# Compressed attention branch of a hybrid decoder block: PSUM copies moved from the vector to the scalar engine, two clamps replaced by a mask column, and low parts placed behind a weight split

## The chip, the cores and the metric

One core of a Trainium2 chip runs the kernel. Its engines work in parallel, each through its own queue in order: TensorE (PE in the profile, its weight loads PEld), VectorE (DVE), ScalarE (ACT), GpSimd (POOL), and SyncE (SP), which issues the DMAs. They are held together by semaphores that are written out by hand. The metric is device time in microseconds for one execution, as the median of several.

## The reference

One mixer layer: RMS norm, one input projection of 512 tokens x 1024 channels, three head groups, and one output projection added to the residual.

```
h = rmsnorm(x, norm_g)
proj = jnp.einsum('bsd,de->bse', h, w_in)
...
y_lru = rglru_group(...)     # gated linear recurrence
y_nsa = nsa_group(...)       # 8 query heads, 2 key/value heads
y_fox = fox_group(...)       # 8 heads, forget gates
y = jnp.concatenate([y_lru, y_nsa, y_fox], axis=-1)
return x + jnp.einsum('bse,ed->bsd', y, w_out)
```

The change touches the compressed branch of `nsa_group`. Its keys and values are made from 31 overlapping windows of 32 tokens. A query may see a window only when the window ends at or before it, so the first 31 queries see none and get zero:

```
k_cmp = rmsnorm(einsum(kc[:, tok] + pe_k, wck), k_g);  v_cmp = einsum(vc[:, tok] + pe_v, wcv)
s = jnp.einsum('bsgrd,bngd->bgrsn', qg, k_cmp) * ATTN_SCALE
s = jnp.where(mask, s, NEG_INF);  m = max(s);  e = jnp.where(mask, jnp.exp(s - m), 0.0)
p = e / jnp.maximum(jnp.sum(e), 1e-30)
o = jnp.einsum('bgrsn,bngd->bsgrd', p, v_cmp)
```

With 512 tokens there are 8 selection blocks of 64 and up to 16 may be selected, so the selected branch takes them all, and the importance scores need not be computed.

## The kernel before, in words

**Precision.** Every fp32 product with a weight is made of three matmuls on split operands: high x high, high x low and low x high. ACT copies a raw weight chunk to its high part (`split`, L513, 128x1024), then DVE subtracts to get the low part (`split_low`, L791). Queries and keys are treated alike: ACT writes the high part (`norm_high`, L589, two halves of 64 partitions), DVE the low part (L815, two halves).

**The stream of chunks.** The input projection runs over 39 chunks of 128 output channels (`CHUNKS`), in this order at the start: `u` x4 (recurrence input), `fg` (gate logits), `kc`, `vc` (input of the compressed keys and values), `ks`, `kw`, `nq` x4 (queries of the NSA group), `vn` x2 (token-major values), `zl` x4 (gates of the recurrence). Then comes the first attention (64 units of scores, exponent, transpose, values; TensorE lines L1232, L1241, L1260), 20 more chunks, the second attention, 4 chunks and the output projection. `project(c)` on TensorE makes a chunk with 24 matmuls (L1146 to L1148; for `vn` four units of 24 with 256 columns, L1126 to L1128). A chunk is read out of one of three PSUM banks, so a unit waits for the read of the unit three before it.

**Each engine has its own loop over the same chunks.** What stands in it by hand is the order of the engine's queue. Names for the order in one iteration `c`, before the change:

- ACT: exponent of the compressed scores (`zl` only, L670), `norm_seeds(c-1)` (four activations L521 to L524), `split(c+3)`, `before(c)` (square L545, or sigmoid L539 for `zl`), the first three reads of a `vn` chunk (`read_tokens`, L603), `norm_high(c-1)`, the fourth read; and after `nq3` the high part of the compressed keys (L704).
- DVE: `cmp_probs(t)` (`zl` only, L906 to L921), the read of chunk `c` (L769), `cmp_values` at `vn0` (L892), `after(c-1)` (L808 to L810 normalise, then the two low parts L815, which wait for ACT's high parts), `lru_tail` (L851 to L856 in two pieces), `cmp_norm` after `nq3` (L880 to L885), `cmp_transposed` (`zl` only, L930), `split_low(c+3)`.
- TensorE: `project(c)`; inside `zl0`, after half of its matmuls, `cmp_scores(0)` (L1192); after each `zl` chunk `t`: `cmp_transpose(t)` (L1201), `cmp_scores(t+1)`, `cmp_values(t)` (L1212). `cmp_transpose(t)` waits for DVE's `cmp_probs(t)`.

**The compressed branch, block t of 128 queries.** TensorE scores against high and low keys into one bank; DVE adds the mask and the two parts, takes the row maximum, clamps it, subtracts; ACT takes the exponent; DVE sums, clamps the sum, multiplies with the reciprocal and the gate; TensorE transposes into `PT[0]`; `cmp_transposed(t)` copies the 128x256 result to `std`; TensorE multiplies with `v_blocks`; `cmp_out_read(t)` copies the 128x512 output to `o_nsa`. `v_blocks` is block-diagonal, filled by `cmp_values` with eight copies of 32x64 out of PSUM. The clamps exist for rows without a visible window:

```
link(dve.tensor_scalar(mx, mx, NEG / 10, None, ALU.max))
link(dve.tensor_scalar(sm, sm, 1e-30, None, ALU.max))
```

`link` makes DVE wait for its own result. The compressed keys and values have 32 columns; column 31 is padding and zero in both. On ACT, sigmoid and the exponent set are in different tables; a switch is an instruction of its own (ACT_TABLE_LOAD).

## Time and profile before

| | |
|---|---|
| median of 3 runs | 458.04 us (457.46 to 458.3) |
| the profiled execution | 459.54 us, its span 457.7 us |
| TensorE, matmul | 434.9 us busy, 95% of the span |
| VectorE | 298.8 us, 65% |
| ScalarE | 255.7 us, 56% |
| GpSimd | 75.5 us, 16% |
| chain that ended last | PE 82%, DVE 9%, issue 3%, ACT 3%, DMA 2% |

The profile follows one execution. The chain of waits goes back from the last instruction, at each step to what released it; its shares tell on which engine the end of the kernel hung. The granted clock of TensorE is given as a share of full speed: 1.00 is 2.4 GHz and 0.50 is 1.2 GHz.

### The profile page before, as it was taken

What the parts mean: (1) busy time and instruction counts of PE and PEld (TensorE: products, weight loads), DVE (VectorE), ACT (ScalarE), POOL (GpSimd) and SP (SyncE); (2) the same over time, 40 slices, a digit from 0 to 9 for tenths busy, and PEclk for the clock granted to TensorE, in tenths of its full rate; (3) what the DMA queues carried; (4) which work ended last, traced back from release to release, by engine and by line L of the source; (5) the groups of instructions that cost most, each with busy time, mean ns of one, the idle gap of its engine ahead of it and who ended that gap; (6) DMA issues with size and microseconds to landing.
All of it is one profiled execution on the core that took longest, in us unless ns stands there. A gap on an engine that the chain in (4) does not pass through costs nothing.

```text
span 457.7 us, 6527 instructions
## 1 busy us (share of the span) xinstructions
PE 434.9 (95%) x2232; PEld 333.5 (73%) x2232; DVE 298.8 (65%) x631; ACT 255.7 (56%) x496; POOL 75.5 (16%) x122
## 2 busy tenths in 40 slices
PE   5899999999859989999999999999799999999997
PEld 1477688777848866676667897898577778888885
DVE  5975549887797998767427863857886448722204
ACT  4645695468734577878718873862487635311100
POOL 3002240000000036666500000000166300000000
PEclk9899999999997999999999999999999999999999
DMA  7822333432121210000011225372400012832004
GB/s 248 328 92 86 99 94 92 139 92 92 47 92 48 92 47 3 1 1 2 1 46 48 92 70 161 95 204 71 134 5 1 1 47 95 280 132 92 1 0 183
DMA packets 12961, 39.52 MB, mean 86 GB/s; under 512 B 1792, under 2 KB 2048, under 8 KB 12672
## 3 DMA queue, kind: packets, MB, share of 16 engines
q1 hardware_dynamic: 12928, 39.11, 26.5%
q8 instruction: 18, 0.29, 0.3%
q14 instruction: 15, 0.12, 0.1%
HBM read 32.81 MB, written 2.10 MB: 76 GB/s over the span
## 4 chain that ended last, share of the span: by engine, by line
PE 82%; DVE 9%; issue 3%; ACT 3%; DMA 2%; SPq 1%; POOL 0%; DVEq 0%; ACTq 0%; POOLq 0%
PE bank L1146 12%; PE bank L1148 12%; PE bank L1147 12%; PE bank L1260 6%; PE bank L1241 6%; PE bank L1363 5%; PE bank L1361 5%; PE bank L1362 5%; PE bank L1232 3%; PE bank L1233 3%; PE bank L1157 2%; PE bank L1126 2%; PE bank L1176 2%; PE bank L1128 2%; PE bank L1127 2%
## 5 line engine op out<-in xcount | busy, mean ns | idle before, releaser
L1146 PE MATMUL bank<-xh,wh 128*128 128x512 f32 (+1 forms) x264 | 112.4, 426 | 0.0
L1148 PE MATMUL bank<-xh,wl 128*128 128x512 f32 (+1 forms) x264 | 104.1, 394 | 0.0
L1147 PE MATMUL bank<-xl,wh 128*128 128x512 f32 (+1 forms) x264 | 103.5, 392 | 0.0
L791 DVE TENSOR_TENSOR wl<-raw,wh 128x1024 fp32r<-128x1024 f32 x51 | 62.0, 1219 | 30.2 <-ACT wh L513 29.8
L513 ACT ACTIVATE wh<-raw 128x1024 fp32r<-128x1024 f32 x51 | 53.0, 1049 | 29.6 <-PE bank L1363 27.0
L1146 PEld LDWEIGHTS bank<-xh,wh 128*128 128x128 f32 (+1 forms) x264 | 49.7, 188 | 14.6 <-issue 4.6
L1147 PEld LDWEIGHTS bank<-xl,wh 128*128 128x128 f32 (+1 forms) x264 | 49.7, 188 | 14.6 <-issue 4.2
L1148 PEld LDWEIGHTS bank<-xh,wl 128*128 128x128 f32 (+1 forms) x264 | 49.3, 187 | 11.8
L987 DVE CUSTOM_DVE_ANT_0 bank<-bank,mask_row 128x256 f32<-128x256 f32 (+3 forms) x96 | 46.8, 499 | 14.0 <-PE bank L1233 13.4
L481 POOL TENSOR_SCALAR probs<-probs,rcp,gates 128x384 f32<-128x384 f32 (+3 forms) x44 | 27.2, 628 | 115.4 <-DVE rcp L1003 115.3
L1363 PE MATMUL bank<-wh,yl 128*128 128x512 f32 x96 | 37.8, 394 | 0.0
L1361 PE MATMUL bank<-wh,yh 128*128 128x512 f32 x96 | 37.8, 394 | 0.0
L1362 PE MATMUL bank<-wl,yh 128*128 128x512 f32 x96 | 37.8, 394 | 0.0
L634 ACT ACTIVATE probs<-bank,negmax 128x256 f32<-128x256 f32 (+3 forms) x64 | 33.7, 530 | 5.3 <-DVE negmax L987 5.2
L644 ACT ACTIVATE pT<-bank 128x384 f32<-128x384 f32 (+1 forms) x48 | 26.1, 546 | 13.3 <-PE bank L1241 12.8
L1241 PE MATMUL bank<-cst,probs 128*128 128x128 f32 x160 | 28.4, 278 | 1.8 <-POOL probs L481 0.8
L1126 PE MATMUL bank<-wh,xh 128*128 128x256 f32 x96 | 28.5, 297 | 1.3 <-ACT v_nsa L603 1.3
L1127 PE MATMUL bank<-wl,xh 128*128 128x256 f32 x96 | 26.8, 280 | 0.0
L1128 PE MATMUL bank<-wh,xl 128*128 128x256 f32 x96 | 26.8, 280 | 0.0
L769 DVE TENSOR_TENSOR qr<-bank,rstd_bc 128x512 f32<-128x512 f32 (+1 forms) x19 | 13.1, 688 | 20.0 <-PE bank L1148 19.9
L1232 PE MATMUL bank<-kh_nsa,q_nsa 128*128 128x256 f32 (+3 forms) x64 | 25.1, 395 | 0.9 <-ACT probs L634 0.9
L1241 PEld LDWEIGHTS bank<-cst,probs 128*128 128x128 f32 x160 | 18.5, 140 | 7.4 <-POOL probs L481 3.3
(208 smaller groups left out, 786.2 us busy)
## 6 DMA issues: line engine op xcount, KB each, us to landing
raw<-in_w_in SPq DMA_DIRECT2D x39, 512.0 KB, 3.4
raw<-in_w_out SPq DMA_DIRECT2D x12, 512.0 KB, 3.4
x_raw<-in_xT SPq DMA_DIRECT2D x8, 256.0 KB, 6.1
x_res<-in_x_tok SPq DMA_DIRECT2D x1, 2048.0 KB, 9.6
out_y<-y_out SPq DMA_DIRECT2D x8, 256.0 KB, 2.1
cmp_w_sb<-in_cmp_w SPq DMA_DIRECT2D x1, 1024.0 KB, 9.9
kh_fox<-kh_fox SPq DMA_DIRECT2D x8, 128.0 KB, 2.3
kl_fox<-kl_fox SPq DMA_DIRECT2D x8, 128.0 KB, 2.4
```

Of the source, the lines that this page charges most:

```text
L513: act.activation(wh[:, c % HL, :], raw[:, c % RAW, :], ACT.Copy).then_inc(wh_ready, 1)
L791: dve.tensor_tensor(wl[:, c % HL, :], raw[:, c % RAW, :], wh[:, c % HL, :].bitcast(F32), ALU.subtract).then_inc(wl_ready, 1)
L987: dve.tensor_tensor_reduce(scores, scores, mask_row[:, SEQ - n:], scale=-1.0, scalar=3.0e38, op0=ALU.add, op1=ALU.min, accum_out=negmax[:, ...
L1126: pe.matmul(dst, xh[:, k, toks], hi[:, k], start=(k == 0), stop=False)
L1146: pe.matmul(dst, hi, xh[:, k, :], start=(k == 0), stop=False)
L1147: pe.matmul(dst, hi, xl[:, k, :], start=False, stop=False)
L1148: mm = pe.matmul(dst, lo, xh[:, k, :], start=False, stop=(k == KT - 1))
L1232: pe.matmul(dst[:, 0:n], q, kh[:, 0:n], start=(group == "nsa"), stop=False)
L1241: mm = pe.transpose(PT[u % PTB][:, cols], probs_of(u, j * P, (j + 1) * P), ident)
L1361: pe.matmul(dst, yh[:, e, toks], wh[:, c % HL, cols], start=(e == 0), stop=False)
L1362: pe.matmul(dst, yh[:, e, toks], wl[:, c % HL, cols], start=False, stop=False)
L1363: mm = pe.matmul(dst, yl[:, e, toks], wh[:, c % HL, cols], start=False, stop=(e == ET - 1))
```

## The change

Four edits. (1) `cmp_values` (8 copies), `cmp_transposed` (4 copies) and `cmp_out_read` (4 copies) go from DVE to ACT. The eight stand behind `split` of iteration `vn0` and ahead of the reads of that chunk; `cmp_transposed(t)` stands behind `split` and ahead of the sigmoid of `zl` chunk `t`; `cmp_out_read(t-1)` stands behind the exponent of block `t`, the last one in step 7 of the first attention. (2) The two clamps go. Instead, the mask's padding column 31 holds -1e29 in place of -1e30: the row maximum is then never under -1e29, and a row without a visible window has its whole weight on the padding column, whose value is zero. (3) On DVE, `after` is cut in two: `split_low(c+3)` now stands between the normalisation and the two low parts (`after_low`), in both loops over chunks. (4) `cmp_scores(0)` stands behind two of the eight channel tiles of chunk `zl0`, not four.

```
@@ -564,6 +564,28 @@
+            def cmp_values():
+                act.wait_ge(v_cmp_T, 1)
+                for g in range(KVH):
+                    for r in range(GROUP):
+                        act.activation(v_blocks[32 * r:32 * r + 32, g, r * HD:(r + 1) * HD],
+                                       AUX_B[0:CMP_PAD, g * HD:(g + 1) * HD], ACT.Copy).then_inc(v_cmp_ready, 1)
+            def cmp_transposed(t):
+                act.wait_ge(cmp_pT, t + 1)
+                if t >= 1:
+                    act.wait_ge(cmp_o, t)
+                act.activation(std[:, 0:2 * P], PT[0][:, 0:2 * P], ACT.Copy).then_inc(cmp_pT_sb, 1)
+            def cmp_out_read(t):
+                act.wait_ge(cmp_o, t + 1)
+                act.activation(o_nsa[:, :, t * P:(t + 1) * P],
+                               OUT[t % 2][:, :].rearrange("p (i q) -> p i q", i=HEADS // 2),
+                               ACT.Copy).then_inc(cmp_o_read, 1)
             def norm_seeds(c):
@@ -637,6 +659,8 @@
                 for s, inside in steps(first, last):
+                    if s == 7:
+                        cmp_out_read(NT - 1)
                     u = inside(s - T_LAG)
@@ -668,9 +692,15 @@
                     act.activation(p, p, ACT.Exp).then_inc(cmp_exp, 1)
+                    if t >= 1:
+                        cmp_out_read(t - 1)
                 if c >= 1:
                 split(c + AHEAD)
+                if CHUNKS[c][0] == "zl":
+                    cmp_transposed(CHUNKS[c][1])
+                if c == AT["vn", 0]:
+                    cmp_values()
                 before(c)
@@ -809,6 +839,10 @@
                                              ALU.mult).then_inc(normed, 1)
+            def after_low(c):
+                if c in NORMED:
+                    n = nth_normed(c)
                     for s in range(2):
@@ -884,13 +918,6 @@
                                       ALU.subtract).then_inc(k_cmp_ready, 1)
-            def cmp_values():
-                dve.wait_ge(v_cmp_T, 1)
-                for g in range(KVH):
-                    for r in range(GROUP):
-                        dve.tensor_copy(v_blocks[32 * r:32 * r + 32, g, r * HD:(r + 1) * HD],
-                                        AUX_B[0:CMP_PAD, g * HD:(g + 1) * HD]).then_inc(v_cmp_ready, 1)
@@ -907,32 +934,16 @@
                 link(dve.tensor_reduce(mx, p3, AX.X, ALU.max))
-                link(dve.tensor_scalar(mx, mx, NEG / 10, None, ALU.max))
                 dve.tensor_tensor(p3, p3, mx.unsqueeze(2).broadcast_to([P, HEADS, CMP_PAD]),
                 if t >= 1:
-                    cmp_out_read(t - 1)
                     lru_output(t - 1)
                 link(dve.tensor_reduce(sm, p3, AX.X, ALU.add))
-                link(dve.tensor_scalar(sm, sm, 1e-30, None, ALU.max))
                 link(dve.reciprocal(rc, sm))
                                   ALU.mult).then_inc(cmp_p, 1)
-            def cmp_transposed(t):
-                dve.wait_ge(cmp_pT, t + 1)
-                if t == 0:
-                    dve.wait_ge(normed, 6)
-                if t >= 1:
-                    dve.wait_ge(cmp_o, t)
-                dve.tensor_copy(std[:, 0:2 * P], PT[0][:, 0:2 * P]).then_inc(cmp_pT_sb, 1)
-            def cmp_out_read(t):
-                dve.wait_ge(cmp_o, t + 1)
-                dve.tensor_copy(o_nsa[:, :, t * P:(t + 1) * P],
-                                OUT[t % 2][:, :].rearrange("p (i q) -> p i q", i=HEADS // 2)).then_inc(cmp_o_read, 1)
@@ -972,8 +983,6 @@
                 for s, inside in steps(first, last):
-                    if s == 7:
-                        cmp_out_read(NT - 1)
                     if s == 16:
@@ -1060,18 +1069,16 @@
                     cmp_out(1)
-                if c == AT["vn", 0]:
-                    cmp_values()
                 if c >= 1:
                     after(c - 1)
+                split_low(c + AHEAD)
+                if c >= 1:
+                    after_low(c - 1)
                 for i, step in enumerate(TAIL_AT):
                     cmp_norm()
-                if CHUNKS[c][0] == "zl":
-                    cmp_transposed(CHUNKS[c][1])
-                split_low(c + AHEAD)
             attention(0, NSA_UNITS)
@@ -1081,6 +1088,7 @@
                 split_low(c + AHEAD)
+                after_low(c - 1)
             attention(NSA_UNITS, UNITS)
@@ -1138,7 +1146,7 @@
                         head_mean(c - 1)
-                    if k == KT // 2 and c == AT["zl", 0]:
+                    if k == 2 and c == AT["zl", 0]:
                         cmp_scores(0)
@@ -1425,6 +1433,7 @@
         c[:, CMPMASK + t * CMP_PAD:CMPMASK + (t + 1) * CMP_PAD] = np.where(seen, 0.0, NEG)
+        c[:, CMPMASK + t * CMP_PAD + N_CMP] = NEG / 10
     return c```

**DVE, from the normalisation of `nq2` to the first mask addition of the compressed branch (iterations `nq3`, `vn0`, `vn1`).** `wl` is the low weight part, `q_nsa` the low query parts, `k_cmp_*` the norm of the compressed keys. Before:

```order
L810 SCALAR_TENSOR_TENSOR qr<-qr,chn,std 128x512
L815 TENSOR_TENSOR q_nsa<-qr,q_nsa 64x512 x2
L880 TENSOR_TENSOR k_cmp_sq<-k_cmp_sq,k_cmp_w 64x64
L881 SCALAR_TENSOR_TENSOR k_cmp_y<-k_cmp_sq,k_cmp_y 64x64
L882 SCALAR_TENSOR_TENSOR k_cmp<-k_cmp,chn,k_cmp_y 64x64
L885 TENSOR_TENSOR k_cmp_parts<-k_cmp,k_cmp_parts 64x2x32 x2
L791 TENSOR_TENSOR wl<-raw,wh 128x1024
L892 COPY v_blocks<-bank3 32x64 x8
L808 TENSOR_TENSOR work<-work,bank5 128x512
L809 SCALAR_TENSOR_TENSOR std<-work,std 128x512
L810 SCALAR_TENSOR_TENSOR qr<-qr,chn,std 128x512
L815 TENSOR_TENSOR q_nsa<-qr,q_nsa 64x512 x2
```

The same place after:

```order
L840 SCALAR_TENSOR_TENSOR qr<-qr,chn,std 128x512
L821 TENSOR_TENSOR wl<-raw,wh 128x1024
L849 TENSOR_TENSOR q_nsa<-qr,q_nsa 64x512 x2
L914 TENSOR_TENSOR k_cmp_sq<-k_cmp_sq,k_cmp_w 64x64
L915 SCALAR_TENSOR_TENSOR k_cmp_y<-k_cmp_sq,k_cmp_y 64x64
L916 SCALAR_TENSOR_TENSOR k_cmp<-k_cmp,chn,k_cmp_y 64x64
L919 TENSOR_TENSOR k_cmp_parts<-k_cmp,k_cmp_parts 64x2x32 x2
L838 TENSOR_TENSOR work<-work,bank5 128x512
L839 SCALAR_TENSOR_TENSOR std<-work,std 128x512
L840 SCALAR_TENSOR_TENSOR qr<-qr,chn,std 128x512
L821 TENSOR_TENSOR wl<-raw,wh 128x1024
L849 TENSOR_TENSOR q_nsa<-qr,q_nsa 64x512 x2
```

The low weight part now stands ahead of the low query parts in both iterations, so ahead of the norm of the compressed keys too, and the eight copies are gone. Between the last row and the mask addition there were five `lru_tail` instructions and two low weight parts; now there are the same five and one.

**ACT, iteration `vn0` to the first exponent of the compressed branch.** `v_nsa` are the token-major reads, `q_nsa` the high query parts. Before:

```order
L524 ACTIVATE bank5<-bank4,half_eps 128x512
L513 ACTIVATE wh<-raw 128x1024
L603 ACTIVATE v_nsa<-bank0,rstd_col 128x256
L603 ACTIVATE v_nsa<-bank1,rstd_col 128x256
L603 ACTIVATE v_nsa<-bank6,rstd_col 128x256
L589 ACTIVATE q_nsa<-qr 64x512 x2
L603 ACTIVATE v_nsa<-bank0,rstd_col 128x256
L513 ACTIVATE wh<-raw 128x1024
L670 ACTIVATE qr<-qr 128x256
```

After:

```order
L524 ACTIVATE bank5<-bank4,half_eps 128x512
L513 ACTIVATE wh<-raw 128x1024
L572 ACTIVATE v_blocks<-bank3 32x64 x8
L625 ACTIVATE v_nsa<-bank0,rstd_col 128x256
L625 ACTIVATE v_nsa<-bank1,rstd_col 128x256
L625 ACTIVATE v_nsa<-bank6,rstd_col 128x256
L611 ACTIVATE q_nsa<-qr 64x512 x2
L625 ACTIVATE v_nsa<-bank0,rstd_col 128x256
L513 ACTIVATE wh<-raw 128x1024
L694 ACTIVATE qr<-qr 128x256
```

The eight copies stand ahead of the reads of `vn0`, for which TensorE waits, and ahead of the high query parts, for which DVE waits.

**ACT, from the exponent of block 3 to the first exponents of the first attention.** `sq<-y_lru` is the sigmoid of chunk `zl3`. Before:

```order
L670 ACTIVATE qr<-qr 128x256
L513 ACTIVATE wh<-raw 128x1024
L539 ACT_TABLE_LOAD
L539 ACTIVATE sq<-y_lru 128x512
L705 ACT_TABLE_LOAD
L634 ACTIVATE probs,rsum<-bank4,negmax 128x256
```

After:

```order
L694 ACTIVATE qr<-qr 128x256
L585 ACTIVATE o_nsa<-bank2 128x4x128
L513 ACTIVATE wh<-raw 128x1024
L580 ACTIVATE std<-bank7 128x256
L539 ACT_TABLE_LOAD
L539 ACTIVATE sq<-y_lru 128x512
L735 ACT_TABLE_LOAD
L656 ACTIVATE probs,rsum<-bank4,negmax 128x256
```

The load of the sigmoid's table stood right behind the weight split; now a copy that waits for TensorE's transpose stands between them, and so it is in each of the four `zl` iterations.

## Rows read from the trace of the kernel before

**Rows 1.** The page, busy time and share of the span, instructions.

```profile
PE 434.9 (95%) x2232; PEld 333.5 (73%) x2232; DVE 298.8 (65%) x631; ACT 255.7 (56%) x496; POOL 75.5 (16%) x122
```

**Rows 2.** Who waited for whom, TensorE: us in total, times, longest.

```profile
PE bank L1231 <- ACT work L634: 2.0, 1, 2.0
...
PE bank L1232 <- ACT probs L634: 0.9, 1, 0.9
```

**Rows 3.** The chain of waits, 100 to 170 us: start, us, what.

```profile
104.64 0.04 DVE qr L769
```

**Rows 4.** Windows, TensorE: length, busy (x instructions), granted clock, DMA share, GB/s.

```profile
132.00:135.00 3.00, 0.00 (x0) 1.00 0.79 242
136.00:142.00 6.00, 5.56 (x22) 0.50 0.29 96
142.00:146.00 4.00, 4.00 (x19) 1.00 0.01 2
330.00:333.00 3.00, 3.00 (x11) 0.50 0.47 157
```

**Rows 5.** Timeline, DVE, 113 to 137 us: start, length, in brackets idle before.

```profile
113.92 0.75 DVE L810 SCALAR_TENSOR_TENSOR qr<-qr,chn,std 128x512 f32<-128x512 f32 x1
115.37 1.39 DVE L815 TENSOR_TENSOR q_nsa<-qr,q_nsa 64x512 fp32r<-64x512 f32 x2 [0.70 <-ACT q_nsa L589]
...
119.81 1.93 DVE L892 COPY v_blocks<-bank 32x64 f32<-32x64 f32 x8
...
124.67 1.39 DVE L815 TENSOR_TENSOR q_nsa<-qr,q_nsa 64x512 fp32r<-64x512 f32 x2 [0.70 <-ACT q_nsa L589]
...
130.14 2.33 DVE L791 TENSOR_TENSOR wl<-raw,wh 128x1024 fp32r<-128x1024 f32 x2
132.39 0.41 DVE L906 TENSOR_TENSOR qr<-bank,cst 128x256 f32<-128x256 f32 x1
...
133.75 0.17 DVE L910 TENSOR_SCALAR cmp_stat<-cmp_stat 128x8 f32<-128x8 f32 x1
...
135.96 0.42 DVE L921 TENSOR_TENSOR qr<-qr,cmp_stat 128x256 f32<-128x256 f32 x1
```

**Rows 6.** Timeline, ACT, 109 to 125 us.

```profile
109.53 0.26 ACT L523 ACTIVATE k_cmp_sq<-k_cmp_y 64x64 f32<-64x64 f32 x1
109.70 0.29 ACT L524 ACTIVATE k_cmp_w<-bank,half_eps 64x64 f32<-64x64 f32 x1
...
117.60 0.54 ACT L704 ACTIVATE k_cmp_parts<-k_cmp 64x64 fp32r<-64x64 f32 x2 [1.61 <-DVE k_cmp L882]
...
120.09 0.64 ACT L524 ACTIVATE bank<-bank,half_eps 128x512 f32<-128x512 f32 x1
...
121.60 1.19 ACT L603 ACTIVATE v_nsa<-bank,rstd_col 128x256 f32<-128x256 f32 x3
124.01 1.29 ACT L589 ACTIVATE q_nsa<-qr 64x512 fp32r<-64x512 f32 x2 [1.21 <-DVE qr L810]
```

**Rows 7.** Timeline, TensorE, 120 to 165 us.

```profile
122.12 0.38 PE L1126 MATMUL bank<-wh,xh 128*128 128x256 f32 x1 [1.35 <-ACT v_nsa L603]
...
127.71 0.97 PE L1192 MATMUL bank<-k_cmp_parts,q_nsa 128*128 128x64 f32 x8
...
136.44 0.69 PE L1201 MATMUL bank<-cst,qr 128*128 128x128 f32 x2 [4.91 <-DVE qr L921]
...
146.62 0.38 PE L1201 MATMUL bank<-cst,qr 128*128 128x128 f32 x2
...
162.22 0.44 PE L1201 MATMUL bank<-cst,qr 128*128 128x128 f32 x2
```

**Rows 8.** Timeline, ACT, at the start of the first attention.

```profile
163.12 0.63 ACT L539 ACTIVATE sq<-y_lru 128x512 f32<-128x512 f32 x1 [1.74 <-DVE y_lru L769]
163.76 1.28 ACT L705 ACT_TABLE_LOAD   x1
165.06 0.47 ACT L634 ACTIVATE probs<-bank,negmax 128x256 f32<-128x256 f32 x1
```

## The prediction, on record before the changed kernel ran

> **What bounds the kernel now.** The page comes first: TensorE is busy 434.9 us of the span [rows 1]. So only its idle stretches can be won, and whatever makes its busy stretches slower. The list of who waited for whom gives the second attention's start, 2.0 us for the first exponent [rows 2]. The largest wait near the change stands in TensorE's timeline: 4.91 us ahead of the transpose of block 0 at 136.44, for DVE's L921, and ahead of it 1.35 us at 122.12 for ACT's reads of `vn0` [rows 7]. The chain of waits tells which counts: at 104.64 it stands on DVE's read of chunk `nq2` [rows 3], which TensorE had just finished, and it comes back to TensorE only at 136.44. In these 31.8 us DVE and ACT hand work back and forth and TensorE has 1.35 + 4.91 = 6.3 us to spare. The windows give the second cost of that wait: TensorE's granted clock is 1.00 in 132 to 135, while it idles, then 0.50 (1.2 GHz) in 136 to 142 and 1.00 again in 142 to 146 [rows 4]. From 136.44 to 146.62, one block with its chunk, it takes 10.18 us; the next two blocks take 15.60, or 7.80 each [rows 7]. So the low clock cost 2.38 us, all of it on the path. From 146.62 on TensorE is the bound until the first attention, where ACT is: sigmoid at 163.12, table load at 163.76, first exponent at 165.06 [rows 8].
>
> The profiled execution took 459.54 us with a span of 457.7. Its own time is 1.50 over the median of the runs, 458.04. I sum differences against the profiled one and take them off the median.
>
> **The change, part by part.**
>
> *DVE up to the low parts of `nq3`.* `nq2` is normalised at 113.92 + 0.75 = 114.67 as before. The low weight part used to follow later; it now runs at once, 2.33 / 2 = 1.17 each, about 1.2 alone [rows 5]. Before, DVE stood 0.70 for ACT's first high part and finished at 115.37 + 1.39 = 116.76 [rows 5]. Now: 114.70 + 1.2 + 1.4 = 117.3, so 0.56 later. The norm of the compressed keys comes behind it, and ACT's L704 waits for that: 117.60 becomes 118.16 [rows 6]. ACT's `norm_seeds(nq3)` is queued behind L704 and ends at 120.09 + 0.64 + 0.56 = 121.29 instead of 120.73 [rows 6]. DVE used to fill this time with 1.2 us of weight split and the eight copies, 1.93 us [rows 5]. They are gone from here, so DVE simply stands still for about 2 us until 121.3. It normalises `nq3` by 121.3 + 2.2 = 123.5, against 124.67 - 0.70 = 123.97 [rows 5]: of the 1.93 us that left DVE, 0.44 is won.
>
> *The eight copies on ACT.* They stand where the reads of `vn0` began: 121.60 + 0.56 = 122.16 [rows 6]. No row shows a 32x64 copy from PSUM on ACT. Below: L524 on 64x64 starts 0.17 behind L523 [rows 6], 8 x 0.17 = 1.4 us. Above: 0.29 for L524 out of PSUM [rows 6] with 0.02 between, 2.5 us. L704 is the nearest, since it is small and changes its partitions from one to the next, and it takes 0.54 / 2 = 0.27 without overlap [rows 6]; DVE's own eight do not overlap either (1.93 / 8 = 0.24) [rows 5]. I take 0.28, or 2.3 us. The three reads then run 124.46 to 125.65 (1.19), the high parts of `nq3` to 125.67 + 1.29 = 126.96 [rows 6]. DVE did its low weight part meanwhile (to 124.7) and waits again; its second low part ends at 126.98 + 0.7 = 127.7 instead of 124.67 + 1.39 = 126.06 [rows 5]. That is 1.64 later.
>
> *From there to the transpose of block 0.* Before, 126.06 to 132.39: `lru_tail` and two low weight parts. One of these is done already, 1.17 less. So L906 starts at 132.39 + 1.64 - 1.17 = 132.86. The two clamps are on the path: 133.95 is 0.20 behind L910's start at 133.75, and the second is like it (L918, same shape); 0.41 together. The last instruction ended at 135.96 + 0.42 = 136.38 [rows 5], now 136.38 + 0.47 - 0.41 = 136.44. **By DVE the transpose is where it was, +0.06.** The copy work taken off DVE comes back as waiting for ACT.
>
> *TensorE ahead of it.* The fourth unit of `vn0` waits for the first read: 122.12 + 0.56 + 2.3 = 124.98. It has been idle since 122.12 - 1.35 = 120.77 [rows 7], 4.2 us. The wait of 4.91 let the clock fall, and so did the 2.0 us of [rows 2], with 0.50 in the window behind it [rows 4]. So I expect 1.2 GHz from about 125 on. It lasted 5.56 us of work in one case [rows 4] and at least the 3 us of the window in the other; half of it is lost, 1.6 to 2.8 us. Up to its end of `zl0`, 136.44 - 4.91 = 131.53 before [rows 7], TensorE needs 9.41 us at full clock. New end: 131.53 + 2.86 + (1.6 to 2.8) = 136.0 to 137.2. So the transpose starts between 136.5 and 137.2; I take **136.8, +0.35**. The move of `cmp_scores(0)` costs nothing: its end was 127.71 + 0.97 - 122.12 = 6.56 behind the start of the unit [rows 7], and six matmuls earlier it is nearer to 5.2. Even with the low clock it is there by 133, when DVE comes to it; without the move it could be a good microsecond late.
>
> *What this gives back.* TensorE now comes to the transpose nearly without a pause, at full clock. The first block takes 7.80, not 10.18: **-2.38**.
>
> *The three next blocks.* DVE loses both copies and both clamps there, but TensorE is the bound (7.80 each) and gets nothing. ACT's chain inside a block: transposes end 0.44 behind their start [rows 7], copy of 128x256 about 0.45, table load 1.28, sigmoid 0.63, table load 1.28, exponent of half a row 0.4 [rows 8]: 4.6 us. Behind it DVE has the recurrence output and the sums, some 2 us. Together 6.6 of 7.80, so it is hidden by 1.2 us.
>
> *Start of the first attention.* Here nothing hides it. Before, the sigmoid's table was loaded ahead of the wait, and the first exponent came 165.06 - 162.22 = 2.84 behind the last transpose [rows 7, 8]. Now: 0.44 + 0.04 + 0.47 for the copy, 1.28, 0.63, 1.28 and three gaps of 0.02, 4.19 us. **+1.35**, with all 64 units of the attention behind it. In step 7 ACT takes the last output copy, about 0.65, which DVE loses at the same place: 0.
>
> *Everything else.* The second loop has the same swap on DVE (low weight part first), but there TensorE has no wait for DVE until the second attention: 0. The mask column costs nothing.
>
> Sum: +0.35 - 2.38 + 1.35 = **-0.7 us**; 459.54 becomes 458.85, and on the median 458.04 - 0.7 = 457.35, say 457.4.
>
> **A rule of the skill against the rows.** Four table loads of 1.28 us lie behind a wait now, two in a row per block. In [rows 8] the sigmoid's end (163.75), the load at 163.76 and the exponent at 165.06 leave 0.03 us beside the load. The Trainium skill, "ScalarE: Activation LUTs", What ACT_TABLE_LOAD costs, gives 1.28 us for the load and some 1.38 us more for a drain at every switch. By that the start of the attention would come 1.38 later for the additional load, and the sum would be -0.7 + 1.38 = +0.7 us. The trace does not agree: there is no room for the drain in 0.03 us.
>
> **The rivals.** What a measurement can tell from no change is 0.2%, 0.9 us.
>
> *A, faster: ACT's copies are short.* At the lower bound of 1.4 us all that hangs on them (reads, high parts, fourth unit) comes 0.9 earlier: -0.7 - 0.9 = -1.6, 456.4. For it speaks that L523 and L524 overlap [rows 6]; against it that L704, on changing partitions, does not. 0.20.
>
> *B, slower: the clock falls at the start of the first attention.* TensorE idled 0.9 us there for the exponent [rows 2] and would idle 2.2. The second attention starts in the same way with 2.0 [rows 2] and has 0.50 afterwards [rows 4]. [...] Price as above 1.6 to 2.8 us, as little is spare behind it: -0.7 + 1.6 to 2.8 = +0.9 to +2.1, 459.0 to 460.1. Against it: TensorE is dense before and the fall need not come at 2 us. 0.17.
>
> *C, the clock does not fall at `vn0`.* Then `zl0` is done at 134.4, the transpose starts at 136.5 after an idle of 2.1 us: -1.0 (457.0) if the clock holds there as well, +0.6 and more (458.7) if it falls. 0.10.
>
> *D, slower: a switch of tables behind a wait takes longer than one ahead of it*, by as much as the load itself, 1.28. One additional load on the path and two in each block, where 1.2 us were spare: +0.6 to +2 in all, 458.6 to 460. Nothing in the rows asks for it. 0.03. The skill's rule on the drain, above, would be of this kind.
>
> *The forecast*, both costs and gains present and nearly even, -0.7 with its own range of -1.5 to +0.2 (458.2 to 456.5), from the 1.2 us of spread in the clock's stretch and 0.4 each in copies and sums: 0.50.
>
> **The numbers.** Of the forecast 0.17 lies beyond -0.9 us, 0.31 within, 0.02 over. Of A 0.19 is faster. Of B 0.13 slower, 0.04 within. Of C 0.05, 0.03, 0.02. D is slower. Faster 0.41, same 0.39, slower 0.20. The range leaves out A's lower end and B's upper: 455.9 to 459.4.
>
> **What the profile after would show.** Right: DVE idle of some 2 us ahead of the normalisation of `nq3` and another ahead of its low parts; eight ACT copies of about 2.3 us; TensorE idle of some 4 us in `vn0` with clock 0.50 behind it; next to no idle and clock 1.00 at the transpose of block 0; all blocks 7.80 apart; first exponent 4.2 behind the last transpose. Wrong: if the copies take under 1.5 us, if 0.50 stands behind either of the later waits, or if blocks are further apart than 7.80, which would mean that ACT's chain isn't hidden.

## The result: slower, by 0.36%

The changed kernel takes 460.55 us (median of 15 runs), the kernel before 458.98 us in 15 runs beside it. The ratio is 1.0036, with an interval of 1.0024 to 1.0049, or about 1.6 us more. The forecast was 457.4 us with a range up to 459.4, so its sign is wrong and the time lies outside its range. The profiled execution of the changed kernel took 461.26 us with a span of 459.5 (before: 459.54 and 457.7, so 1.8 more).

The page, busy time and share of the span; beside [rows 1]:

```profile
PE 435.8 (95%) x2232; PEld 335.2 (73%) x2232; DVE 290.2 (63%) x607; ACT 260.6 (57%) x512; POOL 75.2 (16%) x122
```

DVE lost 8.6 us of work and ACT got 4.9; the edits move copies from one to the other and take the clamps away. That tells nothing of the time. Who waited for whom does (TensorE; us in total, times, longest), beside [rows 2]:

```profile
PE bank L1134 <- ACT v_nsa L625: 3.7, 1, 3.7
PE bank L1240 <- ACT probs L656: 2.4, 1, 2.4
PE bank L1165 <- ACT sq L545: 2.2, 1, 2.2
```

The first two are places of which the forecast spoke. The third, L1165, is in no row of before: TensorE waited for nothing between 19 and 104 us there. It is the head mean of chunk `ks`, at 76.59 us, long ahead of the compressed branch. DVE's timeline shows how it came about (start, length, in brackets the idle time before):

```profile
66.19 0.69 DVE L857 TENSOR_TENSOR head_sel_f<-qr,sq 8x512 f32<-8x512 f32 x1
70.03 1.23 DVE L821 TENSOR_TENSOR wl<-raw,wh 128x1024 fp32r<-128x1024 f32 x1 [3.16 <-ACT wh L513]
...
74.07 1.22 DVE L890 TENSOR_TENSOR_SCAN u_pad<-tau,ig 128x512 f32<-128x512 f32 x1
75.21 0.67 DVE L799 TENSOR_TENSOR qr<-bank,rstd_bc 128x512 f32<-128x512 f32 x1
```

ACT's timeline gives the reason for the 3.16 us (L715 to L723 are the long square-root, logarithm and exponent block of the recurrent branch):

```profile
58.96 2.20 ACT L715 ACTIVATE u_pad<-tau 128x512 f32<-128x512 f32 x4
...
68.34 0.63 ACT L723 ACTIVATE xc<-xc 128x512 f32<-128x512 f32 x1
68.88 1.99 ACT L513 ACTIVATE wh<-raw 128x1024 fp32r<-128x1024 f32 x2
75.91 0.63 ACT L545 ACTIVATE sq<-qr 128x512 f32<-128x512 f32 x1 [5.04 <-DVE qr L799]
```

And TensorE's:

```profile
74.01 0.40 PE L1156 MATMUL bank<-xh,wl 128*128 128x512 f32 x1
76.59 1.13 PE L1165 MATMUL bank<-sq,cst 128*128 128x512 f32 x2 [2.19 <-ACT sq L545]
```

Its windows behind that (length, busy, granted clock, DMA share, GB/s):

```profile
77.00:81.00 4.00, 4.00 (x11) 0.58 0.63 135
85.00:89.00 4.00, 4.00 (x18) 1.00 0.07 16
```

In iteration `vc` the low weight part (L821) now stands ahead of the recurrence's tail (L885 to L890). It needs ACT's high part L513, which is queued behind ACT's long block until 68.88. In the kernel before, DVE used just that time for the tail, its five instructions of 4 us (first of the tail, then the low part behind it):

```profile
66.90 0.69 DVE L851 SCALAR_TENSOR_TENSOR u_pad<-tau,xc 128x512 f32<-128x512 f32 x1
...
70.95 1.20 DVE L791 TENSOR_TENSOR wl<-raw,wh 128x1024 fp32r<-128x1024 f32 x1
```

Now it stands still for 3.16 us, does the tail afterwards, and reads chunk `ks` at 75.21 instead of 72.06; ACT squares it at 75.91, and TensorE, which has the head mean of that square next in its queue, idles 2.19 us and then has its clock at 0.50 in most of 77 to 81. Up to the read of `vc` itself the two kernels agree to the hundredth:

```profile
64.91 0.69 DVE L799 TENSOR_TENSOR kv_cm<-bank,rstd_bc 128x512 f32<-128x512 f32 x1 [4.06 <-PE bank L1156]
...
108.68 0.69 DVE L799 TENSOR_TENSOR qr<-bank,rstd_bc 128x512 f32<-128x512 f32 x1 [2.25 <-PE bank L1156]
```

Before, the first of these reads is at 64.91 too and the second (chunk `nq2`) at 104.64 [rows 3]. So **4.04 us** were lost in this stretch: 2.19 of waiting, and 1.85 behind it, where the clock was low.

Behind it, the places of the forecast. TensorE, beside [rows 7]:

```profile
128.51 0.39 PE L1134 MATMUL bank<-wh,xh 128*128 128x256 f32 x1 [3.70 <-ACT v_nsa L625]
...
139.96 0.44 PE L1209 MATMUL bank<-cst,qr 128*128 128x128 f32 x2 [0.42 <-DVE qr L945]
...
141.04 1.14 PE L1220 MATMUL bank<-std,v_blocks 128*128 128x128 f32 x8
...
147.53 0.38 PE L1209 MATMUL bank<-cst,qr 128*128 128x128 f32 x2
...
162.56 0.38 PE L1209 MATMUL bank<-cst,qr 128*128 128x128 f32 x2
```

Its windows, beside [rows 4]:

```profile
129.00:132.00 3.00, 3.00 (x16) 0.50 0.50 175
...
139.00:141.00 2.00, 1.58 (x13) 1.00 0.02 8
```

ACT in the same stretch and at the start of the first attention, beside [rows 6, 8]:

```profile
126.11 1.85 ACT L572 ACTIVATE v_blocks<-bank 32x64 f32<-32x64 f32 x8
127.98 1.20 ACT L625 ACTIVATE v_nsa<-bank,rstd_col 128x256 f32<-128x256 f32 x3
...
164.67 0.63 ACT L539 ACTIVATE sq<-y_lru 128x512 f32<-128x512 f32 x1
165.32 1.28 ACT L735 ACT_TABLE_LOAD   x1
166.62 0.47 ACT L656 ACTIVATE probs<-bank,negmax 128x256 f32<-128x256 f32 x1
```

The four transposes are 7.57, 7.52 and 7.51 us apart (before 10.18, 7.80, 7.80), and the first exponent comes 4.06 behind the last one (before 2.84). The account of the two profiles, up to the first exponent:

| stretch | before | after | difference |
|---|---|---|---|
| read of `vc` to read of `nq2` | 39.73 | 43.77 | +4.04 |
| to the transposes of block 0 | 31.80 | 31.28 | -0.52 |
| block 0 | 10.18 | 7.57 | -2.61 |
| blocks 1 and 2 | 15.60 | 15.03 | -0.57 |
| to the first exponent | 2.84 | 4.06 | +1.22 |
| sum | | | +1.56 |

Without the first line the change would have won 2.5 us in this pair of profiles.

No run takes edit 1 or edit 4 alone. The profile gives an estimate for edit 4: the scores of block 0 ended at 135.31 and DVE came for them at 136.31. Two more channel tiles ahead of them are 1.37 us (132.97 to 134.34), so without the edit DVE would have waited about 0.4 us.

### The profile page after: what moved, and what is told of

Read it like the earlier page. It is cut to its first block, busy times and chain, and to the rows that moved or that the text cites. A ratio compares the mean times of both kernels' runs of the same rounds, so it can differ in the third digit from the quotient of the medians.

```text
span 459.5 us, 6518 instructions
## 1 busy us (share of the span) xinstructions
PE 435.8 (95%) x2232; PEld 335.2 (73%) x2232; DVE 290.2 (63%) x607; ACT 260.6 (57%) x512; POOL 75.2 (16%) x122
## 4 chain that ended last, share of the span: by engine, by line
PE 77%; DVE 9%; ACT 8%; issue 3%; DMA 1%; SPq 0%; POOL 0%; DVEq 0%; ACTq 0%
PE bank L1154 11%; PE bank L1156 10%; PE bank L1155 10%; PE bank L1268 6%; PE bank L1249 6%; PE bank L1370 5%; PE bank L1371 5%; PE bank L1369 5%; PE bank L1240 3%; PE bank L1241 3%; PE bank L1165 2%; PE bank L1184 2%; PE bank L1136 2%; PE bank L1134 2%; PE bank L1135 2%
## 5 line engine op out<-in xcount | busy, mean ns | idle before, releaser
L1156 PE MATMUL bank<-xh,wl 128*128 128x512 f32 (+1 forms) x264 | 104.7, 397 | 0.0
L821 DVE TENSOR_TENSOR wl<-raw,wh 128x1024 fp32r<-128x1024 f32 x51 | 62.0, 1218 | 35.5 <-ACT wh L513 35.5
L513 ACT ACTIVATE wh<-raw 128x1024 fp32r<-128x1024 f32 x51 | 53.0, 1049 | 29.7 <-PE bank L1371 29.6
L1156 PEld LDWEIGHTS bank<-xh,wl 128*128 128x128 f32 (+1 forms) x264 | 49.8, 188 | 11.9
L656 ACT ACTIVATE probs<-bank,negmax 128x256 f32<-128x256 f32 (+3 forms) x64 | 33.7, 531 | 4.8 <-DVE negmax L996 4.6
L1134 PE MATMUL bank<-wh,xh 128*128 128x256 f32 x96 | 29.0, 302 | 3.7 <-ACT v_nsa L625 3.7
L799 DVE TENSOR_TENSOR qr<-bank,rstd_bc 128x512 f32<-128x512 f32 (+1 forms) x19 | 13.0, 685 | 27.4 <-PE bank L1156 27.4
L1135 PE MATMUL bank<-wl,xh 128*128 128x256 f32 x96 | 27.6, 287 | 0.0
L1240 PE MATMUL bank<-kh_nsa,q_nsa 128*128 128x256 f32 (+3 forms) x64 | 25.1, 395 | 2.4 <-ACT probs L656 2.4
```

The source lines that it names most:

```text
L513: act.activation(wh[:, c % HL, :], raw[:, c % RAW, :], ACT.Copy).then_inc(wh_ready, 1)
L821: dve.tensor_tensor(wl[:, c % HL, :], raw[:, c % RAW, :], wh[:, c % HL, :].bitcast(F32), ALU.subtract).then_inc(wl_ready, 1)
L1134: pe.matmul(dst, xh[:, k, toks], hi[:, k], start=(k == 0), stop=False)
L1156: mm = pe.matmul(dst, lo, xh[:, k, :], start=False, stop=(k == KT - 1))
L1240: pe.matmul(dst[:, 0:n], q, kh[:, 0:n], start=(group == "nsa"), stop=False)
```

## The experiments

The ratios below are to the kernel before, with the 95% interval in brackets. The theory after the result: the whole loss is one place of edit 3, in iteration `vc`. The rivals: the reordering costs elsewhere too; or the loss is in the copies moved to ACT and only looks like this. Absolute times move by about a microsecond between groups of runs (the kernel before has medians of 458.39, 459.23 and 459.16 in them), so the ratio is what to compare.

### Both tail pieces ahead of the low part in `vc`

```
+                if c == AT["vc", 0]:
+                    lru_tail(0, 0)
+                    lru_tail(0, 1)
                 split_low(c + AHEAD)
                 ...
-                    if step == c:
+                    if step == c and c != AT["vc", 0]:
```

> The changed kernel, but in DVE's iteration vc the two pieces of lru_tail(0) stand ahead of split_low again, as in the kernel before; all else stays. Theory W: the loss is there. DVE stood 3.16 us for ACT's high weight part behind split_low, TensorE waited 2.19 us for a square and then ran at 0.50 of its clock; nq2 is read 4.04 us later than before (108.68 against 104.64). Expected 4.0 us under the changed kernel and about 2.4 us under the kernel before (ratio 0.995); no wait of TensorE for the square, nq2 read at 104.6. Rival C: the loss comes from the copies on ACT (eight copies ahead of the vn0 reads, 1.2 us more at the start of the attention). Then this stays 1.6 us over before (ratio 1.0035).

Measured: 456.52 us, ratio 0.9959 (0.9944 to 0.9974), against 1.0036 with the fault: 3.5 us back. TensorE:

```profile
134.82 0.44 PE L1212 MATMUL bank<-cst,qr 128*128 128x128 f32 x2 [0.42 <-DVE qr L945]
...
162.11 0.80 PE L1243 MATMUL bank<-kh_nsa,q_nsa 128*128 128x512 f32 x1 [2.42 <-ACT probs L656]
```

From the read of `vc` (63.81) to that of `nq2` (103.55) it takes 39.74 us, as before the change; the wait at L1165 is gone, and up to the first exponent all behind it is as in the changed kernel (31.27 from the read of `nq2` to block 0, then 7.58). Behind the wait of 2.42 us the clock is low here, which it was not in the profile of the changed kernel:

```profile
162.00:164.00 2.00, 1.89 (x7) 0.50 0.06 25
```

The theory holds; of the 4.0 us that it gave, the runs show 3.5.

### Only the first tail piece ahead

```
+                if c == AT["vc", 0]:
+                    lru_tail(0, 0)
                 split_low(c + AHEAD)
```

> As e1, but only the first piece of lru_tail(0), two of five instructions or 1.45 us, stands ahead of split_low in iteration vc. Theory W with a threshold: DVE then waits about 1.7 us, TensorE had about 1.0 us to spare there, so it waits 0.7 us and its clock stays at 1.00: 0.7 us over e1. Rival P: the loss is in proportion to DVE's delay (1.7 of 3.15 us gives 2.2 of 4.0 us over e1), or the clock falls after 0.7 us as well and about 1.8 us more are lost.

Measured: 458.19 us, ratio 0.9988 (0.9973 to 1.0003), between the two.

```profile
PE bank L1167 <- ACT sq L545: 0.7, 1, 0.7
```

A wait of 0.73 us, and 40.74 us from read to read, 1.0 more than without it. The clock stayed up in the profile, as the theory with a threshold has it; by the ratios the loss is 1.3 us and not 0.7, and the 2.2 of the proportional rival is too much. The runs fall into two groups, five of 456.7 to 457.1 us and seven of 458.0 to 459.0. The mean granted clock of each run is on record, and it parts them without exception: 0.988 or 0.989 in the five, 0.985 or 0.981 in the seven. The profile is of the fast group, so the clock that stayed up in it isn't typical.

### The fault alone, in the kernel before

```
+                if c == AT["vc", 0]:
+                    split_low(c + AHEAD)
                 for i, step in enumerate(TAIL_AT):
                 ...
-                split_low(c + AHEAD)
+                if c != AT["vc", 0]:
+                    split_low(c + AHEAD)
```

> The kernel before, with nothing but split_low ahead of the two pieces of lru_tail(0) in iteration vc. Theory W: the loss alone, +4.0 us (ratio 1.009), nq2 read at 108.7, and it passes through to the end because everything from there to the transpose of block 0 hangs on the read of nq2. Rival C: 0, since no copy is on ACT. Rival S: TensorE's 6.3 us of waits later on swallow part of it, +0 to +2 us.

Measured: 462.3 us, ratio 1.0084 (1.0063 to 1.0104), 3.9 us slower than before by this one transposition.

```profile
68.59 1.22 DVE L791 TENSOR_TENSOR wl<-raw,wh 128x1024 fp32r<-128x1024 f32 x1 [3.15 <-ACT wh L513]
...
107.23 0.69 DVE L769 TENSOR_TENSOR qr<-bank,rstd_bc 128x512 f32<-128x512 f32 x1 [0.72 <-PE bank L1151]
```

The read of `vc` is at 63.48, so 43.75 us lie between the reads: +4.02 against +4.04 in the changed kernel. The copies have no part in it.

### The changed kernel with the old order

```
-                split_low(c + AHEAD)
-                if c >= 1:
                     after_low(c - 1)
                 ...
                 if c == AT["nq", 3]:
                     cmp_norm()
+                split_low(c + AHEAD)
```

and the same in the second loop: edit 3 undone in both.

> The changed kernel with split_low at its old place in both loops over chunks (edit 3 undone; copies on ACT, mask column and earlier scores stay). Theory W: the loss at vc is gone; the swap was worth next to nothing elsewhere, since DVE waits for ACT instead. About 2.0 to 2.4 us under before (ratio 0.995), within 0.4 us of e1. If the swap was worth the two waits of 0.70 us for ACT's high parts on the path, e1 is 1.4 us faster than this. Rival C: still 1.6 us over before.

Measured: 458.66 us, ratio 1.0011 (0.9991 to 1.0031): edits 1, 2 and 4 alone give nothing that can be told from zero. The forecast of 2.0 to 2.4 us under the kernel before failed, and so did the rival of 1.6 over it.

```profile
124.04 0.39 PE L1133 MATMUL bank<-wh,xh 128*128 128x256 f32 x1 [3.23 <-ACT v_nsa L625]
...
136.62 0.44 PE L1208 MATMUL bank<-cst,qr 128*128 128x128 f32 x2 [1.54 <-DVE qr L945]
```

It takes 31.94 us from the read of `nq2` to block 0, 0.67 more than in the first experiment; the medians are 2.1 apart, and where the rest comes from is taken up below. So the reordering, faulty in one place, is worth something in the others.

### The clamps alone

The kernel before without its two clamps, with the mask's padding column instead (edit 2).

> The kernel before with edit 2 alone: the two clamps are gone and the mask's padding column holds -1e29. Theory: 0.4 us is won on the path once, ahead of the transpose of block 0; in the three next blocks TensorE is the bound and gets nothing: 0.4 us under before, hardly to be measured. Rival: the blocks hang on DVE, each loses 0.4 us, 1.6 us under before in all.

Measured: 458.67 us, ratio 0.9991 (0.9973 to 1.0009). TensorE waits 4.50 us at the transpose of block 0 instead of 4.91, the next comes 10.45 later, and the two after that 7.79 and 7.78. The 0.41 us of the forecast is there at the wait; the block behind it, at low clock, is 0.27 longer than before, for a reason that the profile doesn't show. The interval holds the forecast of 0.4 us as well as zero, and the rival's 1.6 us lies outside it.

### The order alone, without its fault

```
+                if c >= 1 and c - 1 in NORMED:
+                    split_low(c + AHEAD)
+                    after_low(c - 1)
                 ...
                 if CHUNKS[c][0] == "zl":
                     cmp_transposed(CHUNKS[c][1])
-                split_low(c + AHEAD)
+                if c == 0 or c - 1 not in NORMED:
+                    split_low(c + AHEAD)
```

in the kernel before, with edit 3 of the second loop as it is. In the first loop this is the new order in the six iterations behind a normalised chunk only (`kw` to `vn0`); in all others, `vc` and the `zl` among them, the low part stays where it was.

> The kernel before with only the change of order, and that only where no low part of a first-loop tile has to wait for the recurrent branch's long block: DVE's iteration vc keeps both tail pieces ahead of the low part. Copies and clamps stay on DVE as before. Theory (the whole loss of the change sat in that one place, and the rest of the reordering is a small gain): the read of nq2 stays at 104.6 us, TensorE waits for nothing between 19 and 104 us, the transpose of block 0 starts about 1.0 us earlier than 136.44 because the transposes of the compressed branch now fill waits that DVE had, and the ratio is about 0.998. Rival (the order is worth nothing by itself without the copies on the scalar engine): the transpose at 136.2 to 136.6 and a ratio of 1.000. Rival (the low parts of the last tiles are late for their products): a new wait of TensorE at nq or vn0 and a ratio over 1.001.

Measured: 457.39 us, ratio 0.9962 (0.9947 to 0.9977), 1.7 us faster.

```profile
122.39 0.38 PE L1135 MATMUL bank<-wh,xh 128*128 128x256 f32 x1 [1.82 <-ACT v_nsa L603]
...
135.04 0.51 PE L1210 MATMUL bank<-cst,qr 128*128 128x128 f32 x2 [3.23 <-DVE qr L925]
...
145.83 0.38 PE L1210 MATMUL bank<-cst,qr 128*128 128x128 f32 x2
```

The window behind the wait of 3.23 us:

```profile
136.00:141.00 5.00, 5.00 (x20) 0.50 0.32 108
```

Read to read (64.72 to 104.45) it is 39.73, as before; block 0 starts 30.59 behind the read of `nq2`, 1.21 earlier than before, since DVE fills its two waits of 0.70 us for ACT's high query parts with weight splits, of which one (1.17) no longer stands ahead of block 0. The clock falls at block 0 as it did, and the blocks behind it are 7.81 and 7.77 apart. More was won than the 1.0 expected. The rest up to the 1.7 us is within the interval, which begins at 1.1.

### The sigmoid tables ahead of the copy

On top of the first experiment, for the +1.22 us at the start of the attention:

```
                 if CHUNKS[c][0] == "zl":
+                    act.preload_act_table_set("sigmoid_and_others")
                     cmp_transposed(CHUNKS[c][1])
```

> e1 (lru_tail(0) ahead of split_low in iteration vc), and in the zl iterations ACT loads the sigmoid's table ahead of the copy that waits for the transpose, not behind it; the copy is in every table. Theory: the 1.28 us load is on the path only at the start of the first attention, where the first exponent stood 4.06 us behind the last transpose; now 2.8 us. Expected 1.2 us under e1 (about 455.3 us, ratio to before 0.993), TensorE's wait for that exponent 1.2 us instead of 2.4 us. Rival: in the blocks too ACT's chain limits TensorE, then the steps of 7.52 us shorten and the gain is up to 5 us; or the attention is bound by something behind it and nothing is won.

Measured: 454.21 us, ratio 0.9909 (0.9884 to 0.9934), the fastest of all, 4.2 us under the kernel before.

```profile
155.52 1.28 ACT L701 ACT_TABLE_LOAD   x1
157.82 0.38 ACT L580 ACTIVATE std<-bank 128x256 f32<-128x256 f32 x1 [1.01 <-PE bank L1213]
...
160.27 0.47 ACT L656 ACTIVATE probs<-bank,negmax 128x256 f32<-128x256 f32 x1
```

The load now runs in the time in which ACT waits for the transposes, with 1.01 us still to spare. TensorE's wait for the first exponent falls from 2.42 to 1.21 us, and its clock stays up behind it:

```profile
161.00:162.00 1.00, 0.95 (x4) 1.00 1.00 377
```

More was won than the 1.2 us expected. The rival with shorter blocks is out: they are 7.79, 7.51 and 7.51 us apart. The first is even 0.21 longer than without the preload (7.58), since ACT waited only 0.94 us for those transposes, less than the 1.28 of the load.

### Preload with the old order

The same line in the changed kernel with the old order (the fourth experiment).

> The changed kernel with the order of the kernel before (as the run e4) and with the sigmoid tables loaded ahead of the compressed branch's copies (as the run e5). Theory (the two effects add): the load of 1.28 us leaves the start of the first attention, TensorE's wait for the first exponent falls from 2.4 to 1.2 us and its clock stays at full speed there, so the time is 1.3 to 2.3 us under that of e4, and the transpose of block 0 lies 31.9 us behind the read of nq2 as there. Then what stands between this run and e5 is what the corrected order is worth, 0.7 us by the profiles. Rival (order and preload cover the same wait): this run is as fast as e5, 454.2 to 454.6 us.

Measured: 456.82 us, ratio 0.9957 (0.9936 to 0.9979), against 1.0011 without the preload (2.5 us) and 0.9909 with the corrected order (2.2 us). The two effects add. By the profile's waits the preload should give 1.2 and the order 0.7; the rest is in no wait, and this profile shows where some of it lies. TensorE:

```profile
135.40 0.44 PE L1209 MATMUL bank<-cst,qr 128*128 128x128 f32 x2 [1.54 <-DVE qr L946]
144.78 0.38 PE L1209 MATMUL bank<-cst,qr 128*128 128x128 f32 x2
...
163.29 0.50 PE L1240 MATMUL bank<-kh_nsa,q_nsa 128*128 128x512 f32 x1 [1.23 <-ACT probs L656]
```

Its windows:

```profile
137.00:140.00 3.00, 3.00 (x13) 0.57 0.51 171
...
165.00:168.00 3.00, 3.00 (x12) 0.50 0.00 0
```

The clock fell behind the wait of 1.54 us, where it had stayed at 1.00 in the profile without the preload, and the block took 9.38 us instead of 7.58. It also fell behind the wait of 1.23, where it had stayed up in the run with preload and corrected order. So "its clock stays at full speed there" was wrong for this execution.

### The eight copies behind the reads

To shorten the 3.7 us wait in `vn0`, the copies go behind ACT's first reads and high query parts, again on top of the first experiment:

```
-                if c == AT["vn", 0]:
-                    cmp_values()
                 before(c)
                 read_tokens(c, 0, MIDDLE)
                 ...
                     norm_high(c - 1)
+                if c == AT["vn", 0]:
+                    cmp_values()
```

> e1, with ACT's eight v_blocks copies (1.85 us) behind the high parts of nq3, so neither the vn0 reads nor the high parts wait for them. DVE's low parts come 1.1 us earlier and so does the transpose of block 0, counted from the read of nq2 (31.3 us in e1, 30.2 us here). Theory K (the clock decides): TensorE waits 1.9 us at vn0 instead of 3.7 us, ends zl0 early at full clock and then idles some 2.9 us ahead of the transpose; its clock falls there, where all work is on the path, and the result is 0 to 1.3 us over e1. Rival D (the DVE and ACT chain decides): 1.1 us under e1.

Measured: 458.5 us, ratio 0.9989 (0.997 to 1.0009): slower than the first experiment by 1.4 us in the ratio (0.9944 to 0.9974 there, so the two intervals overlap by a hair). Who waited for whom:

```profile
PE bank L1212 <- DVE qr L945: 2.8, 1, 2.8
...
PE bank L1137 <- ACT v_nsa L625: 1.8, 1, 1.8
```

TensorE's window behind the wait of 2.8 us:

```profile
134.00:139.00 5.00, 5.00 (x21) 0.50 0.33 108
```

The wait in `vn0` is 1.9 us shorter and block 0 starts 1.1 earlier (30.17 behind the read of `nq2`). But TensorE now idles 2.8 us at block 0, and the low clock lies behind that wait, where nothing is spare: the first exponent comes 60.04 behind the read of `nq2` against 57.94, 2.1 later. The same edit on top of the preload:

> e5 and e6 together. By theory K 1.2 us under e6, so at or above e5; by rival D the fastest of all, 2.3 us under e1 (about 454.2 us).

Measured: 456.91 us, ratio 0.9956 (0.9937 to 0.9975), against 0.9909 without it. The waits are 1.8 and 2.8 again, and the clock falls behind the second. Twice the same answer by the runs. This profile is of the fastest of the 12 executions (454.82 us), and it is only 0.6 us behind the one with the preload alone.

## Why the prediction was wrong

The step that failed is the paragraph *Everything else*, with its sum of 0. It costed the swap of `split_low` where the second loop has it and in the iterations around the compressed branch, and took the other iterations of the first loop for free. It never asked what stood behind the swapped instruction in `vc`: five instructions of the tail, the read of `ks`, and TensorE behind that. The trace of before had all that was needed: ACT's block until 68.9, the low part on DVE at 70.95 and the tail ahead of it from 66.90. It cost 4.04 us in the profile, 3.9 by the experiment with the fault alone, and the repair gave 3.5. With it the sum would have been +3.3, not -0.7. Measured are +1.8 in the pair of profiles and +1.6 by the runs, since the other terms together came to -2.5 up to the first exponent: the transposes of block 0 are 0.87 earlier than forecast, the three blocks 0.80 shorter, the start of the attention 0.13 shorter. So the gains were sized too low, and what they gave beyond the forecast hid nearly half of what the wrong step cost.

The other steps, with times behind the read of `nq2` where the profiles are shifted:

- *The eight copies on ACT*, 2.3 us: they took 1.85, 0.23 each, so near to DVE's 0.24; L704 (0.27) was the wrong neighbour, and the lower bound of 1.4 was not reached either.
- *DVE's waits*: "about 2 us until 121.3" was 2.12 us until 121.23 (125.27 less the shift of 4.04); a second one of 1.12 ahead of the low parts. Right.
- *TensorE ahead of block 0*: idle of 4.2 was 3.70, and the clock fell behind it as said, to 0.50 in 129 to 132. Rival C is out for this profile. The transposes came at -0.52 instead of +0.35. From 128.51 to 139.96 TensorE took 11.45 us, 0.42 of it waiting for DVE, so 11.03 where the full clock needs 9.41: the low clock cost 1.62, the lower end of the 1.6 to 2.8 taken for it. And DVE, which came last, was half a microsecond earlier than forecast, as the copies were 0.45 shorter.
- *What this gives back*: -2.38 was -2.61. Right, with clock 1.00 in 139 to 141.
- *The three next blocks*, 0: each is 0.28 shorter. TensorE was the bound, but not fully: it waited inside each block for the copy of the transposed probabilities, in gaps too short for the list of waits. DVE's copy stood behind the read of the chunk in its queue; it ended at 147.83 and the value products began at 147.89, 1.27 us behind the transposes at 146.62:

```profile
147.42 0.41 DVE L930 COPY std<-bank 128x256 f32<-128x256 f32 x1
...
147.89 1.16 PE L1212 MATMUL bank<-std,v_blocks 128*128 128x128 f32 x8
```

ACT had nothing else to do there, and the value products began 1.03 behind the transposes at 147.53:

```profile
147.95 0.38 ACT L580 ACTIVATE std<-bank 128x256 f32<-128x256 f32 x1 [2.03 <-PE bank L1209]
...
148.56 1.14 PE L1220 MATMUL bank<-std,v_blocks 128*128 128x128 f32 x8
```

The clamps alone (7.79, 7.78) and the order alone (7.81, 7.77) leave the step as it was; the changed kernel with the old order has 7.52 and 7.50. What is left is edit 1, and the 0.24 between 1.27 and 1.03 says that in it the copy is what counts.
- *Start of the first attention*: +1.35 was +1.22. Right, and the preload takes it away again.
- *Rival B*, the clock falling there: not in the profile of the changed kernel, whose idle was 2.42 us (1.00 in 162 to 167), but in that of the first experiment, behind the same 2.42. So it came in one of these two profiles, and a chance of 0.17 was rather low.
- *The second loop's swap*: no new wait of TensorE for DVE stands in the lists, and the first attention and all behind it are as long as before to 0.3 us in the two profiles, from the first exponent on (292.9 and 292.6), so its 0 was right.

The rule of the Trainium skill ("ScalarE: Activation LUTs", What ACT_TABLE_LOAD costs) on a drain of some 1.38 us at each switch has a second test here, the order sigmoid, load, exponent behind a wait: from 164.67 + 0.63 = 165.30 to the load at 165.32 and from its end at 166.60 to the exponent at 166.62 are 0.02 us each. The trace does not show the drain.

One thing is left: the corrected order is worth 2.2 to 2.4 us by the runs but 0.7 by the waits of the profiles, and the preload 2.3 to 2.5 against 1.2. The rest goes with the clock. Two pairs of profiles show where. From the first exponent to the end of the span it is 293.5 us in the first experiment, with the clock low behind the wait of 2.42, and 292.1 with the preload: 1.4 of the 2.6 us between the two spans. (At the second attention too the clock is low twice as long in the first experiment, in 325 to 333, as with the preload, in 325 to 329.) And of the 3.5 us between the preload with the old and with the corrected order, 0.65 lie ahead of block 0, 1.59 in block 0 and 1.10 behind the first exponent; the last two are the places where the clock fell in one and not in the other.

A profile is one execution, but the mean granted clock is on record for every run. In the twelve profiles this mean is 0.992 where the clock fell twice, 0.989 where it fell three times, 0.984 or 0.985 for four and 0.981 for five, with a low stretch of double length counted as two falls. The runs by their mean clock:

| kernel | 0.991 or more | 0.987 to 0.989 | 0.984 or 0.985 | under 0.984 |
|---|---|---|---|---|
| before (23 runs beside the first experiments) | 0 | 13 | 10 | 0 |
| changed | 0 | 3 | 3 | 9 |
| both tail pieces ahead | 0 | 3 | 3 | 0 |
| old order | 0 | 0 | 7 | 5 |
| preload | 4 | 1 | 0 | 0 |
| preload, old order | 1 | 4 | 3 | 2 |
| copies late | 0 | 0 | 6 | 6 |
| preload, copies late | 1 | 4 | 5 | 2 |

So shorter waits, and waits at the right place, go with fewer falls of the clock over executions, and not only in one, though some rows have few runs. What that is in time is an estimate: from the old order to the corrected one the mean goes from 0.9828 to 0.9868, or 1.8 us of full clock in some 456, and with the wait of 0.7 that is 2.5 where the runs show 2.4. From there to the preload it is another 1.9 and 1.2, or 3.1 for 2.3 measured; not each fall is on the path. What stays open is at which place the clock fell in each execution without a profile.

## What to carry to other kernels

When an edit swaps two steps inside a loop, walk through every iteration of it, not only the one it was made for: for each, ask what the step that moved ahead waits for, and what now stands behind it. An iteration in which another engine has a long block is where it goes wrong; here one iteration of the loop cost 4.0 us and the rest of the swap won 1.7 by itself and 2.2 to 2.4 beside the other edits. Of a wait that can't be avoided, ask also where it stands: an idle of 3.7 us ahead of work with something to spare was cheaper than one of 1.8 us there and 2.8 at the point where each microsecond counts. And a table load goes ahead of the wait, not behind it, if what waits runs under either table and the wait is at least as long as the load.

## What the runs showed of the hardware

- The fall of TensorE's clock is not fixed by the length of the idle time alone. Behind 2.8 to 4.9 us in `vn0` and at block 0 it fell each time, and so it did both times behind 2.2 us in `ks` and in all twelve profiles behind 2.0 us at the second attention; behind 1.9 to 2.0 us at 15 us of the program it fell in five of twelve. Behind 2.42 us at the start of the first attention it stayed up in three profiles (the changed kernel, with one tail piece ahead, with the old order) and fell in two others (with both pieces ahead, and with the late copies). Behind 1.8 us in `vn0` it stayed up three times. Behind 1.5 us it stayed up three times (1.54 at block 0 with the old order; 1.54 and 1.53 in `vn0` with the fault alone and with the clamps alone) and fell once, behind 1.2 us it stayed up twice and fell once, and behind 0.7 us in `ks` it stayed up. So one profile doesn't tell what such a wait costs on the average.
- After a fall the engine runs at 0.50 (1.2 GHz) though it has dense work, for some 3 to 7 us, and is at 1.00 again afterwards (77 to 81, then 85 to 89 in the changed kernel; 136 to 142, then 142 to 146 before). The Trainium skill, "TensorE: Matmul & The Clock Gate", What's actually happening, has it so: the throttled state is the default, and activity releases it. The trace agrees with the release. A default it doesn't show: in the first 3 us of the kernel before, where TensorE has done nothing yet, its granted clock stands at 1.00.
- In 15 to 20 us of the program the clock falls in some executions and not in others, and this shifts the read of `vc`: 64.7 to 65.0 us in the five profiles where it fell, 63.4 to 63.9 in the seven where it didn't. Two profiles are therefore best compared from a common instruction on.
- Copies of 32x64 from PSUM take ACT 0.23 us each in a row of eight, and DVE 0.24.
